# Cached keys, values and states of the sample streams: from SP's queue and a staging ring to transfers on GpSimd's queue that round on the way

## The reference, cut to what matters

```
h = rms_norm(x); q_a,k_a,v_a, q_g,k_g,v_g, r_g, a_lo = split(h @ w_in)
o_att  = softmax(q_a k_a^T / sqrt(128) + bias) v_a       # 8 heads; keys: own chunk and 512 past rows
o_gla  = recurrence S_t = diag(a_t) S_{t-1} + k_t^T v_t ; o_t = q_t S_t    # 4 heads, S is 128 x 256
x = x + rms_norm(concat(o_att, rms_norm(o_gla) * silu(r_g)) @ w_o)
gate, val = split(rms_norm(x) @ w_up);  x = x + rms_norm((silu(conv3(gate)) * val) @ w_down)
```

## Time and profile before

| what | us |
|---|---|
| median of 3 runs (lowest, highest) | 6721.76 (6713.4, 7092.37) |
| the profiled execution's own time | 6715.98 |
| its span on core 4, the slowest | 6714.9 |
| the spans of the eight cores | 6661.3 to 6714.9 |
| TensorE matmuls busy in the span | 6102.4 (91%) |
| VectorE, ScalarE, GpSimd busy | 2672.6, 1740.5, 314.4 |
| mixer stage of tile 4 (with samples) | 315.60 |
| mixer stage of tiles 5, 6, 7 (384 columns, no samples) | 193.40, 192.40, 191.30 |

### The profile page before, as it was taken

One profiled execution on the slowest core, in us unless ns is written; L12 is line 12 of the kernel. 1 busy time (PEld: TensorE's weight loads), 2 busy tenths in 40 slices (PEclk: granted clock), 3 DMA queues, 4 the chain that ended last, 5 costly groups with the idle time before them and its releaser, 6 DMA issues.

```text
span 6714.9 us, 91958 instructions; the slowest of 8 cores (6661.3 to 6714.9 us)
## 1 busy us (share of the span) xinstructions
PE 6102.4 (91%) x33070; PEld 3235.3 (48%) x33412; DVE 2672.6 (40%) x4680; ACT 1740.5 (26%) x2772; POOL 314.4 (5%) x1160
## 2 busy tenths in 40 slices
PE   6879899898999999899967999899989989998997
PEld 3434345343454445444444455555656565554443
DVE  3343233433334433353333543443444335433532
ACT  2222113221133212331122321321332233223310
POOL 1011000010000000000000100000000000000000
PEclk9989999999999999999988999999999999999999
DMA  9979983899737796444564456457556745754443
GB/s 199 212 152 184 192 218 107 197 207 220 226 120 213 208 244 202 148 163 158 196 217 160 179 197 218 167 205 238 194 186 207 254 159 205 244 197 152 163 158 137
DMA packets 214673, 1276.44 MB, mean 190 GB/s; under 512 B 24192, under 2 KB 45584, under 8 KB 86992
## 3 DMA queue, kind: packets, MB, share of 16 engines
q1 hardware_dynamic: 175376, 1008.93, 43.4%
q0 software_dynamic: 37184, 257.79, 20.7%
q10 hardware_dynamic: 1664, 3.81, 0.2%
HBM read 1275.76 MB, written 184.30 MB: 217 GB/s over the span
## 4 chain that ended last, share of the span: by engine, by line
PE 72%; DMA 15%; DVE 6%; ACT 3%; issue 3%; SPq 0%; DVEq 0%; POOL 0%; ACTq 0%; POOLq 0%
PE ps L533 47%; PE ps L1368 12%; DMA sb_RW<-wall 6%; PE ps L1018 6%; DMA sb_xring<-xt 5%; DMA wb<-sb_RW 2%; PE ps L1260 1%; PE ps L1174 1%; PE ps L644 1%; DVE sb_RB L1237 1%; PE ps L649 1%; PE ps L673 1%; DMA yt<-sb_RB 1%; DMA sb_xring<-cv 1%; DMA sb_RC<-x1d 1%
## 5 line engine op out<-in xcount | busy, mean ns | idle before, releaser
L533 PE MATMUL ps<-sb_RC,sb_RW 128*128 128x512 bf16 (+2 forms) x13530 | 2689.6, 360 | 105.7 <-DMA sb_RW<-wall 51.5
L533 PEld LDWEIGHTS ps<-sb_RC,sb_RW 128*128 128x128 bf16 x13680 | 1340.5, 98 | 1456.1 <-issue 147.9
L1368 PE MATMUL ps<-sb_RA,sb_RW 128*128 128x512 bf16 (+2 forms) x6266 | 1258.3, 362 | 54.9 <-DMA sb_RW<-wall 37.2
L533 PE MATMUL ps<-sb_RD,sb_RW 128*128 128x512 bf16 (+2 forms) x4528 | 1018.7, 372 | 138.0 <-ACT sb_RB L1158 65.9
L1368 PEld LDWEIGHTS ps<-sb_RA,sb_RW 128*128 128x128 bf16 x6336 | 624.3, 99 | 691.2 <-issue 92.1
L533 PEld LDWEIGHTS ps<-sb_RD,sb_RW 128*128 128x128 bf16 x4608 | 450.3, 101 | 583.7 <-issue 231.1
L1305 ACT ACTIVATE sb_RD<-sb_RD,sb_convw 128x512 f32<-128x512 f32 (+2 forms) x440 | 322.4, 733 | 1111.1 <-DVE sb_RD L1295 1036.3
L1295 DVE TENSOR_TENSOR sb_RD<-ps,sb_R 128x512 f32<-128x512 f32 (+1 forms) x378 | 238.7, 631 | 843.6 <-PE ps L533 843.6
L1192 DVE TENSOR_SCALAR sb_RB<-ps,sb_cols 128x512 f32<-128x512 f32 (+2 forms) x288 | 200.9, 698 | 869.1 <-PE ps L1368 473.8
L1018 PE MATMUL ps<-sb_RW,sb_RD 128*128 128x256 bf16 (+1 forms) x4224 | 495.0, 275 | 13.3 <-DMA sb_RW<-wall 7.7
L1308 DVE SCALAR_TENSOR_TENSOR sb_RD<-sb_RD,sb_convw 128x512 f32<-128x512 f32 (+2 forms) x440 | 286.7, 652 | 442.0 <-ACT sb_RD L1305 437.4
(11 more groups left out here) (182 smaller groups left out, 3578.4 us busy)
## 6 DMA issues: line engine op xcount, KB each, us to landing
sb_RW<-wb SPq DMA_DIRECT2D x660, 1024.0 KB, 5.8
sb_RW<-wall POOLq DMA_DIRECT2D x168, 1024.0 KB, 21.6
wb<-sb_RW SPq DMA_DIRECT2D x92, 1024.0 KB, 14.9
sb_RW<-wb SPq DMA_DIRECT2D x55, 768.0 KB, 6.2
sb_xring<-xt SPq DMA_DIRECT2D x64, 512.0 KB, 9.9
sb_RA<-xt SPq DMA_DIRECT2D x24, 1024.0 KB, 14.7
x1d<-sb_RB POOLq DMA_DIRECT2D x20, 1024.0 KB, 4.4
sb_RC<-x1d SPq DMA_DIRECT2D x40, 512.0 KB, 7.4
```

Source lines behind the costliest of these rows:

```text
L533: P(lambda: nc.tensor.matmul(ps[:, 0:nt], lhsT=slab[:, kc, c0:c0 + 128], rhs=rhs[:, kc, 0:nt], start=(kc == 0), stop=(kc == NKC - 1)), rd= ...
L1368: P(lambda: nc.tensor.matmul(ps[:, 0:nt], lhsT=slab[:, kc, c * 128:(c + 1) * 128], rhs=act[:, fc, :], start=(fc == 0), stop=(fc == NFC - 1 ...
```

## The change

The keys and the values of a head pair are each loaded by one transfer on POOL's queue from f32 in memory to bf16 in the ring, with no staging and no copies; `samp_load` then gives 12 empty steps in place of 16. The host lays the cached values out with the past block outermost and the stream next, so that a partition's 4,096 values are in the order of the ring. A head's state is asked for on POOL's queue: those of heads 0 and 1 in `after_tail`, ahead of the two biases, which move to POOL's queue too; those of heads 2 and 3 right behind the write of the state of two heads before, whose place they take. That write moves from SP to POOL as well. `xring` is no longer used by the samples.

```diff
-                    K.dma(K.sp, c_sg[h % 2], so, d_sg[h], wr=bso)
                     sv = so.rearrange("p (i v) -> p i v", i=4)
                     yield
...
-                    K.dma(K.sp, c_s4o[h % 2], gs_o[h], so, rd=bso)
+                    K.dma(K.pool, c_s4o[h % 2], gs_o[h], so, rd=bso)
+                    if h < 2:
+                        K.dma(K.pool, c_sg[h], so, d_sg[h + 2], wr=bso)
                     yield
...
         def samp_load(hp):
 
-            for i in range(8):
-                s = s4n[0]
-                s4n[0] += 1
-                so, bso = stage4(s)
-                if i < 4:
-                    K.dma(K.sp, c_s4[s % 2], so, d_ck[hp][:, i * 1024:(i + 1) * 1024], wr=[bso])
-                    copy_av(kTr[:, 2 * i:2 * i + 2, 512:1024], so.rearrange("p (a k) -> p a k", a=2), [bso], [B_kTs])
-                else:
-                    q = i - 4
-                    K.dma(K.sp, c_s4[s % 2], so, d_cv[hp][:, q * 1024:(q + 1) * 1024], wr=[bso])
-                    copy_av(vr[:, 4:8, q * 256:(q + 1) * 256], so.rearrange("p (k n) -> p k n", k=4), [bso], [B_vts])
-                yield
+            K.dma(K.pool, c_ck, kTr[:, :, 512:1024], d_ck[hp].rearrange("p (a k) -> p a k", a=8), wr=[B_kTs])
+            K.dma(K.pool, c_cv, vr[:, 4:8, :], d_cv[hp].rearrange("p (k n) -> p k n", k=4), wr=[B_vts])
+            for _ in range(12):
                 yield
...
-                        K.dma(K.sp, c_bS2[0], biasS, d_biasS.rearrange("p (h k) -> p h k", h=8), wr=[B_R[0]])
-                        K.dma(K.sp, c_bS2[1], biasN, d_biasN.rearrange("p (h k) -> p h k", h=8), wr=[B_ratt[1]])
+                        for i in range(2):
+                            K.dma(K.pool, c_sg[i], stage_s[i][0], d_sg[i], wr=stage_s[i][1])
+                        K.dma(K.pool, c_bS2[0], biasS, d_biasS.rearrange("p (h k) -> p h k", h=8), wr=[B_R[0]])
+                        K.dma(K.pool, c_bS2[1], biasN, d_biasN.rearrange("p (h k) -> p h k", h=8), wr=[B_ratt[1]])
...
-        m["cv"] = c_(cv.transpose(3, 2, 0, 1, 4).reshape(4, 128, 4096))
+        m["cv"] = c_(cv.transpose(3, 2, 1, 0, 4).reshape(4, 128, 4096))
```

More of the change, by code:

```diff
@@ L867, in build_program @@
         c_vst = [K.chan(out=True), K.chan(out=True)]
-        c_s4 = [K.chan(), K.chan()]
+        c_ck, c_cv = K.chan(), K.chan()
         c_sg = [K.chan(), K.chan()]
@@ L871, in build_program @@
         c_s4o = [K.chan(out=True), K.chan(out=True)]
-        s4n = [0]
         oint = acc[:, :].rearrange("p (h x) -> p h x", h=4)
@@ L875, in build_program @@
         biasN = ratt[1][0:NS, :].rearrange("p (h k) -> p h k", h=8)
-        def stage4(i):
-            return xring[:, 2 * (i % 2):2 * (i % 2) + 2, :].rearrange("p a b -> p (a b)"), B_x4[i % 2]
-        B_x4 = [Buf("x4_0"), Buf("x4_1")]
         def samp_load(hp):
-            for i in range(8):
-                s = s4n[0]
-                s4n[0] += 1
-                so, bso = stage4(s)
-                if i < 4:
-                    K.dma(K.sp, c_s4[s % 2], so, d_ck[hp][:, i * 1024:(i + 1) * 1024], wr=[bso])
-                    copy_av(kTr[:, 2 * i:2 * i + 2, 512:1024], so.rearrange("p (a k) -> p a k", a=2), [bso], [B_kTs])
-                else:
-                    q = i - 4
-                    K.dma(K.sp, c_s4[s % 2], so, d_cv[hp][:, q * 1024:(q + 1) * 1024], wr=[bso])
-                    copy_av(vr[:, 4:8, q * 256:(q + 1) * 256], so.rearrange("p (k n) -> p k n", k=4), [bso], [B_vts])
-                yield
+            K.dma(K.pool, c_ck, kTr[:, :, 512:1024], d_ck[hp].rearrange("p (a k) -> p a k", a=8), wr=[B_kTs])
+            K.dma(K.pool, c_cv, vr[:, 4:8, :], d_cv[hp].rearrange("p (k n) -> p k n", k=4), wr=[B_vts])
+            for _ in range(12):
                 yield
@@ L1099, in after_tail @@
                         inherit([B_Sbs], PD2)
-                        K.dma(K.sp, c_bS2[0], biasS, d_biasS.rearrange("p (h k) -> p h k", h=8), wr=[B_R[0]])
-                        K.dma(K.sp, c_bS2[1], biasN, d_biasN.rearrange("p (h k) -> p h k", h=8), wr=[B_ratt[1]])
+                        for i in range(2):
+                            K.dma(K.pool, c_sg[i], stage_s[i][0], d_sg[i], wr=stage_s[i][1])
+                        K.dma(K.pool, c_bS2[0], biasS, d_biasS.rearrange("p (h k) -> p h k", h=8), wr=[B_R[0]])
+                        K.dma(K.pool, c_bS2[1], biasN, d_biasN.rearrange("p (h k) -> p h k", h=8), wr=[B_ratt[1]])
             if samp:
                 inherit(B_kst, B_csq)
-                inherit(B_x4, B_xr)
                 inherit([B_kTs], [x for bb in B_kT for x in bb[4:]])
@@ L1375, in run_tile @@
                 if m2 == 0 and ti + 1 < len(TILES):
-                    if samp:
-                        inherit(B_xr, B_x4)
                     lanes[0].append(norm1_sep(ti + 1))
```

## The result

| kernel | us, profiled or timed | ratio to the kernel before (95%) |
|---|---|---|
| before, first comparison | 6713.4, 6721.8 | |
| changed, first comparison | 6644.6, 6648.2, 6648.9 | 0.9895 (0.9867 to 0.9924) |
| changed, two later comparisons | 6652.3 to 6669.7; 6634.8 to 6648.7 | 0.9907 (0.9880 to 0.9934); 0.9909 (0.9881 to 0.9937) |

The change makes the kernel about 1% faster; the forecast was 1.1%. All three intervals exclude 1, so a difference of 1% could be told from none, finer than the 2% that the prediction allowed. Runs in which some cores had a lower granted clock throughout (three of the changed kernel's six in the first comparison) are left out, and of the profiled run of the changed kernel, where that held for cores 0 to 3, only cores 4 to 7 are read (clock 0.97, spans 6608.1 to 6641.9 us).

A forecast was written before the change was run, and what follows sets the result against it. Copies waiting for transfers were taken to hold up TensorE in tile 4's mixer stage. 204.8 work + 25.6 idle + 9.2 bias + 3 clock = 242.6 us, 73 less than 315.6, so 6716 - 73 = 6643 us; range 6622 to 6688.

The forecast's parts named there:

- The mechanism: Tile 4's mixer stage: copies awaiting transfers hold ScalarE and VectorE, delaying evacuations TensorE needs; 65.7 us of its gaps.
- 25.6 idle: Tile 4's mixer stage: TensorE's remaining idle time, in us, taken as the average of tiles 5 to 7.
- 9.2 bias: Wait for the biases behind two states on POOL after the tail: 2.1 us of issues, 7.1 us of landing.
- 3 clock: Slow matmuls left in the stage: two or three gaps, each with 1.3 us behind it, 3 us.
- The work at full clock: TensorE's work in tile 4's mixer stage: 225.5 us busy less 20.7 us of slow-clock excess, 204.8 us.
- rival A: POOL's queue slow for states and bias: 13 us more at the bias, gain only 40 us, 6676 us; chance 0.20.
- the test that no other stage moves by 10 us: Sign of being wrong: a stage other than tile 4's mixer stage moves by more than 10 us.
- no PE gap over 5 us but one: Sign of being right: TensorE's only large gap is at L907, ended by `biasN`, 9 to 14 us.
- a key load: Key transfer on POOL for later pairs: 22.4 us, inside a cover of 33 us at pair 1.
- The longer state chain: POOL, heads 2 and 3: write landing 3.0 us, load 6.7, with two issues 10.8 us, against 20 us cover.
- B: Rival: transfers are the bound, DMA share above 0.9 in the stage, time stays 6716 us; chance 0.05.
- C: Rival: keys land too late at `att_sample(1)`; gain gone at 63 us landing, slower beyond; chance 0.05.

The follow-up runs named there:

- e5_copies_on_pool: The kernel before with only the 32 staging-ring copies moved from ScalarE and VectorE to GpSimd; tile 4's mixer stage 276.2 us at the median, one run, 6652.2 us.
- e0_after: The changed kernel run once more, unchanged, against the kernel before; ratio 0.9907, tile 4's mixer stage 256.8 us at the median.
- e9_after_again: The changed kernel run again, unchanged, in a later comparison with the kernel before; ratio 0.9909, tile 4's mixer stage 256.1 us.

## Where the prediction was right, and the step that failed

**The mechanism.** It was right. The gaps that name VectorE and ScalarE came from copies that waited for transfers, as the earlier trace rows were read: `e5_copies_on_pool` shows it. What came late next was the bias, as forecast.

**The step that failed** is in the sum: what TensorE still loses in the stage once the transfers' waits go. The terms 25.6 idle + 9.2 bias + 3 clock = 37.8 us measured 31.7 + 11.6 + 8.2 = 51.5 us on core 4, so the stage took 256.3 us and not 242.6. Two terms were mis-sized most: the idle time, taken over from tiles 5 to 7 with the states' waits at nothing, by 6.1 us, and the clock, with the short waits at nothing, by 5.2. The work at full clock is the forecast's 204.8.
- Idle time beside the bias: 43.3 - 11.6 = 31.7 in place of 25.6 (median of 20 cores of three runs of the changed kernel 32.3). The prediction had the states' waits go altogether; 4.8 us of the 14.2 stay, in three waits of at most 2.4, the same on all these cores. They are waits for the copy itself, ahead of which VectorE had no idle time. The trace of before had it already: of its four state copies only two had waited for a transfer, and the other two of TensorE's waits, 1.68 and 2.98 us on all eight cores, were not for a transfer. The copy's line L789 there (what ended its idle time, us, times):

```profile
  DMA sb_RB<-sg: 8.2, 2
```

  And L685 costs 5.4 where tile 5 had 3.71.
- Clock: 213.0 - 204.8 = 8.2 in place of 3 (median of the 20 cores 8.6). Behind the gaps of slab 6 the rows show 1.3 and 1.5 us of slow matmuls, about what was counted. The rest stands behind short waits, which were put at nothing. TensorE later in the stage, columns as in the earlier trace rows, and the granted clock (0.50) in the last of these rows, columns as in the earlier trace rows:

```profile
3455.48 3.06 PE L533 MATMUL ps<-sb_RD,sb_RW 128*128 128x448 bf16 x8
...
3465.27 2.65 PE L533 MATMUL ps<-sb_RD,sb_RW 128*128 128x448 bf16 x8
...
3483.64 8.56 PE L1004 MATMUL ps<-sb_RW,sb_RD 128*128 128x256 bf16 x64
...
3503.52 3.15 PE L533 MATMUL ps<-sb_RD,sb_RW 128*128 128x448 bf16 x8 [2.27 <-ACT sb_RB L1145]
```

```profile
3503.52:3506.67 3.15, 3.15 (x9) 1.31 (x10) 2.48 (x4) 0.29 (x1) 0.00 (x0) 0.50 0.82 299
```

  Just ahead of the four rows TensorE had waited 2.0, 1.2, 2.4 and 2.3 us. Eight matmuls of 448 columns take 1.69 us elsewhere in this stage, and 64 of 256 columns some 7.1 at the pace of tile 5 (96 in 10.64 us), so these rows hold 1.37 + 0.96 + 1.47 + 1.46 = 5.3 us of slow matmuls.
- Bias: 11.6 in place of 9.2. The four issues took 2.2 us as forecast (2.1), the landing 9.9 in place of 7.1. This is rival A in small, 2.8 us and not 13. Over the 20 cores the wait was 9.7 us at the median, near the forecast, so this term failed on core 4 more than in general. The place behind a megabyte of states costs some of it: `biasN` landed in 8.0 us there, in 6.2 ahead of them and in 5.6 where it was asked for in the tile before (medians over the cores).

**The time came out nearer than the stage.** 6643 us were forecast and 6644.6 to 6648.9 measured in the first comparison, a ratio of 0.9895 where 6643 to 6716 is 0.989. But the stage fell by 63 us between the medians of the cores (59.3 on core 4, which had the shortest stage of the eight before), not by 73. That the time came nearer is luck, as far as the runs tell: the three ratios alone stand for some 61 to 71 us of 6716, and cores and runs of one kernel differ by more than the 10 us that are missing. Core 4 began tile 4 at 3326.6 us before and at 3285.6 after, core 5 at 3293.5 and 3308.5; the mean of that start over the eight cores is 3311.8 in `e0_after` and 3292.0 in `e9_after_again`, the same kernel. So the test that no other stage moves by 10 us was too sharp: tile 0's later stages moved by 18 us on core 4, where core 4 and core 5 of one run of before already differ by 10. Tile 4's other stages took 469.5 us before and 469.4 after.

**What would show it.** Met: no copy from the ring, the stage between 223 and 260 us, the clock above 0.9, pair 0 in tile 3's down projection, keys landing between 8 and 25 us (on core 4; pair 0's took up to 30.4 on a core of `e0_after`). Missed: "no PE gap over 5 us but one". Three are there, around the tail's last steps. The first and the last trade: over the 20 cores, where the wait at L1017 is 5.8 or 5.9 us the bias costs 10 to 16, where it is 9.8 or more the bias costs 7.9 to 9.4.

**Keys and states.** 22.4 us were taken for a key load, 10.3 were measured in the stage. On core 4 the keys were asked for 36.5, 54.4 and 48.3 us ahead of their first matmul, where 33, 50 and 34 had been counted. The longer state chain, head 2's, was 0.54 + 3.90 + 7.6 = 12.0 us (issue of the write, wait for it, landing of the load) against a forecast of 10.8 and a cover of 20; no load of heads 2 and 3 was waited for.

**The rivals.** B: the share rose to 0.58, in the shortest version to 0.61, with all the gain kept, so bandwidth was to spare. C would have needed 63 us of landing; eight runs per partition cost nothing that shows in it (10.3 us to the values' 11.1, which have one). The page rule that was given as another way into C (the Trainium skill, "SBUF — State Buffer", "SBUF: two separate sides") isn't seen here either: the POOL issues above took 0.53 to 0.93 us each. Whether VectorE was in the mode that the page names during one of them, the trace does not tell. Two of the prediction's sums were loose: rival A's 12 us are a third of 33 us of waits, where the waits that it names add up to 21; and the range's low end, 6622, asks for some 13 us less idle time than the neighbours have, which "a few" does not say.

## What to carry to other kernels

When a gap names a vector engine, look at what that engine's instruction waited for: a copy that waits for a transfer costs what stands behind it in order, not its own microsecond, and here moving it to an idle engine was already 44 of 57 us of the cure. Small transfers that gate compute go ahead of large ones on their queue, and into memory that no late write still holds. Before a gain is summed, take the stage from several cores, look at each wait for what it will still be when the transfer is gone, and expect slow matmuls behind short waits too.

## What the runs showed that I had not expected

A transfer of 1,024 runs of 1 KB was issued by POOL in 0.89 to 0.93 us, one of 128 runs of 8 KB, as large, in 0.54 to 0.62, and landed as fast (10.3 and 11.1 us). In tile 4's stage a rounding load of 1 MB thus lands in half of the median in the earlier trace rows. Pair 0's two, issued in tile 3's down projection, took longer; their landing, keys and values of all four pairs on core 4 (the longest is pair 0's):

```profile
DMA to landing us min/median/max: 9.6/11.5/16.3
DMA to landing us min/median/max: 9.6/11.4/23.0
```

The share of the DMA engines was 0.9 around them (3133 to 3167 us), where the stage has 0.58. GpSimd rounds 128x1024 values in 1.06 to 1.08 us, as fast as ScalarE's 1.04 and not much behind VectorE's 0.69.
